# Attention in a one-core streaming encoder step: a place for each query block's probabilities, two blocks' scores in one piece, and stage A's transposes by 64 rows in an order by tiling mode

## The reference

```
layer A, prompt:  s = q k^T / 8, per head two components c (64 wide), mask by chunks of 64
                  p = softmax(s);  pd = p[c=0] - lam * p[c=1];  o = pd v   (v 128 wide)
layer A, streams: the same against 512 cached keys and 16 new ones, for 8 streams
                  o = rms_norm(o, g_sub) * 0.8;  x += o w_o
layer B, prompt:  s = q k^T / 8 + f_q - f_k, causal; p = softmax(s); o = p v  (16 heads of 64)
layer B, streams: the same against 512 cached keys and 16 new ones
```

## Time and profile before

| | |
|---|---|
| median of 3 runs | 2539.45 us (2537.55 to 2542.49) |
| the profiled execution | 2543.26 us |
| its span | 2541.5 us |
| PE busy | 2486.0 us, 98% of the span |
| PE weight loads busy | 2351.7 us, 93% |
| DVE busy | 1689.7 us, 66% |
| ACT busy | 1137.5 us, 45% |
| DMA | 271.42 MB, mean 107 GB/s |
| granted PE clock | 0.996 of full speed in the mean |

### The profile page before, as it was taken

The page is one execution under the profiler, slowest core; times in us unless marked ns, Lnnn a source line. Parts: engine busy times, 40 slices in busy tenths (PEclk is TensorE's granted clock), DMA queues, the critical chain, the costliest instruction groups (busy, mean ns, idle before and its releaser), DMA issues.

```text
span 2541.5 us, 46165 instructions
## 1 busy us (share of the span) xinstructions
PE 2486.0 (98%) x18533; PEld 2351.7 (93%) x18533; DVE 1689.7 (66%) x2953; ACT 1137.5 (45%) x2244; POOL 192.5 (8%) x136
## 2 busy tenths in 40 slices
PE   8999999999998999999999999999998899999998
PEld 8999999887777999999988999999985599999998
DVE  7777677331677877767634885868626677858585
ACT  6444344102775634344422543535427755435254
POOL 0000000543000000000054000000120000000000
PEclk9999999999999999999999999999999999999999
DMA  4323232234653222323224232322358731322222
GB/s 127 96 65 102 61 99 66 83 108 136 254 200 101 63 88 73 94 69 98 67 72 138 94 107 67 98 78 79 103 179 310 245 108 43 108 80 77 86 71 79
DMA packets 267136, 271.42 MB, mean 107 GB/s; under 512 B 13786, under 2 KB 224035, under 8 KB 266931
## 3 DMA queue, kind: packets, MB, share of 16 engines
q1 hardware_dynamic: 261184, 253.45, 32.0%
q10 hardware_dynamic: 5746, 15.12, 1.6%
HBM read 255.02 MB, written 13.51 MB: 106 GB/s over the span
## 4 chain that ended last, share of the span: by engine, by line
PE 89%; DVE 5%; ACT 4%; issue 2%; DMA 1%; DVEq 0%; SPq 0%; ACTq 0%
PE PS L775 40%; PE PS L881 24%; PE PS L962 10%; PE PS L725 6%; PE PS L708 2%; PE PS L1208 1%; PE PS L1016 1%; ACT R L1695 1%; PE PS L1147 1%; PE PS L713 1%; DMA R<-in_cache_b_k_dram 1%; ACT R L1727 1%; DVE x_area L2120 1%; PE PS L1168 1%; PE PS L1106 0%
## 5 line engine op out<-in xcount | busy, mean ns | idle before, releaser
L775 PE MATMUL PS<-x_area,w_area 128*128 128x320 f32 x3096 | 482.2, 309 | 0.0
L775 PEld LDWEIGHTS PS<-x_area,w_area 128*128 128x128 f32 x3096 | 461.1, 188 | 0.2 <-DVE w_area L2061 0.2
L881 PE MATMUL PS<-r_area,w_area 128*128 128x320 f32 x2568 | 393.4, 309 | 0.0
L881 PEld LDWEIGHTS PS<-r_area,w_area 128*128 128x128 f32 x2568 | 380.6, 188 | 0.8 <-DVE r_area L2253 0.8
L1482 ACT ACTIVATE w_area<-R 128x512 fp32r<-128x512 f32 x341 | 212.8, 628 | 201.1 <-PE PS L775 134.0
L2052 DVE TENSOR_TENSOR w_area<-R,w_area 128x768 fp32r<-128x768 f32 (+2 forms) x143 | 132.4, 926 | 220.3 <-ACT w_area L1467 218.7
L2061 DVE TENSOR_TENSOR w_area<-R,w_area 128x512 fp32r<-128x512 f32 x341 | 234.0, 687 | 47.4 <-ACT w_area L1482 41.5
L1467 ACT ACTIVATE w_area<-R 128x768 fp32r<-128x768 f32 (+2 forms) x143 | 117.0, 818 | 309.2 <-PE PS L881 281.2
L881 PE MATMUL PS<-v_area,w_area 128*128 128x320 f32 x1620 | 253.5, 309 | 0.0
L962 PE MATMUL PS<-w_area,xn_hi 128*128 128x512 f32 x800 | 251.0, 395 | 0.0
L881 PEld LDWEIGHTS PS<-v_area,w_area 128*128 128x128 f32 x1620 | 241.5, 188 | 0.3 <-DVE v_area L2253 0.3
(11 more groups left out here) (305 smaller groups left out, 3621.9 us busy)
## 6 DMA issues: line engine op xcount, KB each, us to landing
R<-in_w_ffn_up_dram SPq DMA_DIRECT2D x88, 512.0 KB, 3.8
R<-in_w_ffn_gate_dram SPq DMA_DIRECT2D x84, 512.0 KB, 3.9
R<-in_w_ffn_down_dram SPq DMA_DIRECT2D x96, 384.0 KB, 3.3
vreg<-in_cache_a_v_dram SPq DMA_DIRECT2D x8, 2048.0 KB, 8.9
vreg<-in_cache_b_v_dram SPq DMA_DIRECT2D x8, 2048.0 KB, 9.3
R<-in_cache_a_k_dram SPq DMA_DIRECT2D x14, 1024.0 KB, 5.8
R<-in_cache_b_k_dram SPq DMA_DIRECT2D x14, 1024.0 KB, 9.6
R<-in_w_qkv_a_dram SPq DMA_DIRECT2D x24, 512.0 KB, 3.8
```

Source lines behind the costliest of these rows:

```text
L775: last = pe.matmul(PS[:, bank, 0:HT], a[:, k, :], b[:, k, :], start=(start and k == 0 and a is hi and b is x_hi), stop=(k == 3 and a is lo ...
L881: last = pe.matmul(out[:, h, :], a[slot][:, w], x[:, h * HT:(h + 1) * HT], start=(k == 0 and a is w_hi and x is hi), stop=(k == n - 1 and ...
```

## The change

- `probs[x]` becomes a function of the block: each of the four blocks has a place of its own for probabilities, so `exps` no longer waits for the turn of an earlier block. `st` grows by two rows for the same reason, so that blocks 2 and 3 have their own statistics.
- The scores of blocks 0 and 1 of a head are written in one piece (columns 0 to 127 and 128 to 383 of banks 0 and 1), with one semaphore wait, and `peaks(h, (0, 1))` takes both with one `tensor_scalar`.
- Stage A turns probabilities (`turn`), stream differences (`stream_turn`, `stream_turn_new`) and cached keys (`key_pair`, two heads at once) by 64 rows, as B did. ACT takes half of A's `new_differences`. `keys`, `key` and `bank7_uses` go.
- The order of the steps changes on PE, ACT and DVE in both stages. In A PE does full-height work (`output_flips`, `output_rows`, `stream_flips`) in one group, then the 64-row work.
- Some semaphores are merged (`heads_read`, `pd_read`). SP's order is unchanged.

```diff
-        probs = {"A": R2[:, 4096:6144].rearrange("p (s c k) -> p s c k", s=2, c=2),
-                 "B": R2[:, 6144:8192].rearrange("p (s c k) -> p s c k", s=2, c=2)}
+        def probs(x, t):
+            at = {"A": 3584, "B": 6144}[x] + P * t * (t + 1)
+            return R2[:, at:at + 2 * P * (t + 1)].rearrange("p (c k) -> p c k", c=2)
+        def row_stats(t):
+            return st[:, t if t < 2 else t + 2, :]
+        def score_columns(t):
+            return slice(P, 3 * P) if t == 1 else slice(0, (t + 1) * P)
...
 PE, turn:
                     for c in parts:
                         for k in range(t + 1):
-                            block = PR[:, t % 2, c, k * P:(k + 1) * P]
-                            if x == "A":
-                                last = flip(PS[:, 5 + t % 2, k * P:(k + 1) * P], block)
-                                continue
                             at = (c * (t + 1) + k) * 64
                             for r in range(2):
-                                last = half_flip(PS[:, 5 + r, at:at + 64], block, r)
+                                last = half_flip(PS[:, 5 + r, at:at + 64], probs(x, t)[:, c, k * P:(k + 1) * P], r)
...
 PE, stream_turn and stream_turn_new:
+                def stream_block(to, g, k, r):
+                    p, rows = (t0, t1)[g][:, key_block(g, k)], slice(64 * r, 64 * r + 64)
+                    out = PS[:, 2 + 2 * r, to:to + 64]
+                    if x == "A":
+                        return pe.matmul(out, p[rows], Cm[rows, g, rows], start=True, stop=True)
+                    return half_flip(out, p, r)
...
 PE, order in A:
                     for i in range(PAIR):
                         stream_scores(i)
-                        keys(i + 1, 0)
-                        output_rows(i - 1, (0, 1, 2))
+                        output_flips(i - 2)
+                        output_rows(i - 1)
+                        stream_flips(i - 1)
+                        prompt_scores(x, i, (2,))
                         turn(i, 0)
-                        stream_flips(i - 1)
-                        scores(i, 1)
-                        keys(i + 1, 1)
-                        output_rows(i - 1, (3,))
-                        keys(i + 1, 2)
-                        scores(i, 2)
-                        keys(i + 1, 3)
+                        key_pair(i + 1, 0)
                         stream_turn(i)
-                        keys(i + 1, 4)
                         turn(i, 1)
-                        scores(i, 3)
+                        key_pair(i + 1, 1)
+                        prompt_scores(x, i, (3,))
                         stream_turn_new(i)
-                        keys(i + 1, 5)
                         turn(i, 2)
-                        keys(i + 1, 6)
+                        key_pair(i + 1, 2)
                         stream_values(i)
-                        keys(i + 1, 7)
-                        scores(i + 1, 0)
+                        key_pair(i + 1, 3)
+                        prompt_scores(x, i + 1, (0, 1))
                         turn(i, 3)
-                        output_flips(i - 1)
 ACT, order in A:
                     for i in range(PAIR):
+                        stream_roots(i - 1)
                         turned(i - 1, 3)
-                        exps(i, 0)
-                        stream_roots(i - 1)
-                        key(i + 1, 0)
-                        if i == 0:
-                            key(i + 1, 1)
+                        if i:
+                            exps(i, 0)
+                            exps(i, 1)
                         stream_exps(i)
-                        if i > 0:
-                            key(i + 1, 1)
-                        exps(i, 1)
+                        squares(i - 1)
                         turned(i, 0)
-                        key(i + 1, 2)
-                        squares(i - 1)
-                        key(i + 1, 3)
+                        key_pair(i + 1, 0)
+                        differences(i)
                         exps(i, 2)
+                        turned(i, 1)
                         roots(i - 1)
-                        differences(i)
-                        key(i + 1, 4)
-                        turned(i, 1)
-                        key(i + 1, 5)
+                        key_pair(i + 1, 1)
+                        new_differences(i)
                         turned(i, 2)
                         exps(i, 3)
-                        key(i + 1, 6)
+                        key_pair(i + 1, 2)
                         result(i)
-                        key(i + 1, 7)
+                        key_pair(i + 1, 3)
                         stream_squares(i)
 ACT, order in B (after):
                     for i in range(PAIR):
+                        turned(i - 1, 3)
+                        exps(i, 2)
                         stream_exps(i)
                         turned(i, 0)
                         key_pair(i + 1, 0)
-                        exps(i, 2)
                         differences(i)
...
                         exps(i + 1, 0)
+                        exps(i + 1, 1)
                         result(i)
                         key_pair(i + 1, 3)
 DVE, order in A:
                     for i in range(PAIR):
+                        stream_scale(i - 1)
+                        combine(i, 0)
+                        stream_peaks(i)
+                        combine(i, 1)
                         output_columns(i - 2)
-                        combine(i, 0)
-                        stream_scale(i - 1)
-                        stream_peaks(i)
+                        output_rows(i - 1)
                         stream_output(i - 1)
-                        peak(i, 1)
                         stream_norms(i)
-                        output_rows(i - 1)
-                        combine(i, 1)
-                        peak(i, 2)
+                        peaks(i, (2,))
+                        differences(i)
                         sums(i - 1)
-                        differences(i)
                         combine(i, 2)
                         scale_rows(i - 1)
-                        peak(i, 3)
+                        peaks(i, (3,))
                         new_differences(i)
                         combine(i, 3)
                         result(i)
-                        peak(i + 1, 0)
+                        peaks(i + 1, (0, 1))
 DVE, order in B:
                     for i in range(PAIR):
+                        peaks(i, (2,))
+                        stream_peaks(i)
                         combine(i, 1)
-                        stream_peaks(i)
+                        combine(i, 2)
                         output_columns(i - 1)
                         stream_output(i - 1)
-                        peak(i, 2)
                         stream_norms(i)
                         differences(i)
-                        combine(i, 2)
-                        peak(i, 3)
+                        peaks(i, (3,))
                         new_differences(i)
-                        peak(i + 1, 0)
+                        peaks(i + 1, (0, 1))
                         combine(i, 3)
+                        result(i)
                         combine(i + 1, 0)
-                        result(i)
-                        peak(i + 1, 1)
```

More of the change, by code:

```diff
@@ L1007, in first_keys, with prompt_scores @@
                 last.then_inc(sem("kt_ready" + x), 1)
-            def prompt_scores(x, h, t):
-                n = h * 4 + t
+            def prompt_scores(x, h, blocks):
+                if h == PAIR:
+                    return
+                n = h * 4 + blocks[0]
                 if n >= 1:
                     pe.wait_ge(sem(("exp_done" if x == "A" else "nb_ready") + x), n)
[L1014 to L1020, removed]
-                    if x == "A":
-                        last = pe.matmul(out, mask(M_EYE0, P, rows), mask(M_CHUNKED, P, rows), start=False, stop=True)
-                    else:
-                        pe.matmul(out, mask(M_EYE0, P, rows), mask(M_CAUSAL0, P, rows), start=False, stop=False)
-                        last = pe.matmul(out, mask(M_EYE1, P, rows), mask(M_CAUSAL1, P, rows), start=False, stop=True)
-                last.then_inc(sem("s_ready" + x), 1)
@@ new lines, in prompt_scores @@
+                for t in blocks:
+                    at = score_columns(t)
+                    for c in range(2):
+                        rows = slice(64 * c, 64 * c + 64)
+                        pe.matmul(PS[:, c, at], qh[rows, h, t * P:(t + 1) * P], kT[rows, h, 0:(t + 1) * P], start=True, stop=False)
+                    for c in range(2):
+                        rows = slice(64 * c, 64 * c + 64)
+                        out = PS[:, c, at.stop - P:at.stop]
+                        if x == "A":
+                            last = pe.matmul(out, mask(M_EYE0, P, rows), mask(M_CHUNKED, P, rows), start=False, stop=True)
+                        else:
```

(6 more changed lines are left out.)

297 lines of the change are left out of this document (108 added, 189 removed).

## The result

The changed kernel is slower: 2562.56 us in the median of 4 runs (2555.72 to 2564.06), against 2539.53 us for the kernel before on the same chip, a ratio of 1.0084 with a 95% interval of 1.0064 to 1.0105. The forecast was 2531 us, range 2517 to 2546: wrong in sign, and the time lies outside the range. The profiled execution took 2563.2 us.

What follows compares the result with a forecast made beforehand. PE was taken to be near its limit in stage A, and hand-offs to bound B. A -9.5 and B +1 make -8.5 us, 2534.8 from the profiled 2543.26, so 2531 us against the median; range 2517 to 2546.

Steps and rivals of the forecast that it cites:

- PE's work in A: falls by 4.0 us an iteration, from 18.9 to 14.9: First attention stage: half flips and fewer tiling-mode changes cut PE's busy time per iteration by 4.0 us.
- the bound of 0.056 us a pass: A's `stream_turn`: half of 0.112 us, no overlap, giving no gain; the prediction took 0.033 us, giving -0.9 us.
- keys and `turn`: PE in A, full flips to half flips: keys -1.5 us and `turn` -0.5 us per iteration.
- the 1.1 of the mode changes: PE in A: seven fewer tiling-mode changes per iteration at 0.16 us each, -1.1 us.
- The walk of A: 8.3 + 6.0 + 4.1 = 18.4: A's hand-offs from S (start of `stream_scores`) to the next S: period 18.4 us, -1.07 us per iteration.
- The middle term: A, from `stream_turn` to `stream_values`: 6.0 us after the change, 6.07 before.
- First iteration -2.8, last 0: A's ends: first iteration 2.8 us shorter, without earlier output in its path; last unchanged, at worst +0.5.
- B: +1 us: Second attention stage, where only the order moves: later `turn(i, 0)`, some stalls covered; +1 us, bounds -4 and +7.
- B loses more than A gains: Rival, chance 0.13: at `turn(i,0)` ACT is dry, B pays +13 us; with A at -5, 2547 us.
- Clock: Rival, chance 0.04: a quarter of PE's 119 us in A runs at 1.2 GHz, +20 us, 2550 us.
- Sum: Both attention stages: A -9.5 us plus B +1 us, -8.5 us in all.
- three engines at 14 us in 19.5: A after the change: PE, ACT and DVE each hold 14 to 15 us of 19.5, so hand-offs set the period.

Runs made afterwards that it cites:

- The plain turn: On the kernel with fillers, stage A's stream blocks turned by plain 64-row transposes, the product with `Cm` left out; 2537.95 us, ratio 0.9989.
- fillers: Changed kernel plus 128x128 matmuls that nobody reads, where TensorE is idle in both attention stages; 2550.27 us, ratio to before 1.0036.
- moving the two copies: Changed kernel with `output_columns` and `stream_output` directly behind `stream_peaks` on VectorE in B, ahead of two combines; 2548.38 us, ratio 1.0027.
- The last run: Changed kernel, B's old order, fillers at A's ends, block 2's exps first, A's DVE and ACT ordered by PE's waits; 2532.09 us, ratio 0.9963.

## Why the prediction was wrong, step by step

- *PE's work in A: falls by 4.0 us an iteration, from 18.9 to 14.9.* Direction right, size off. One iteration has 16.3 us of PE busy (690.20 to 710.09) where 18.9 stood. The keys came as forecast (sixteen half flips in 0.71 us). `stream_turn` gave nothing: 1.84 us from start to next against 1.79, forecast 0.9. The number of the bound of 0.056 us a pass was right and I chose the other one, on the ground that the operand shapes were the flips'; that bound's reason, no overlap, was not right, for two 64-row passes fit into the time of one full-height pass (0.116 us). Of the 2.6 us that PE's work fell, keys and `turn` were priced at 2.0, so some 0.6 are left for the 1.1 of the mode changes, which no run took apart.
- *The walk of A: 8.3 + 6.0 + 4.1 = 18.4.* Measured 8.52, 7.16 and 4.21. The middle term failed, by the 0.9 us of `stream_turn`; the rest of the walk was within 0.25 us a term. The plain turn bounds what it is worth: at most 0.92 us an iteration and 5.4 over the stage.
- *First iteration -2.8, last 0.* Measured +0.85 and +3.8. With fillers they are -1.9 and +1.8. So the clock took 2.7 us of the first and 2 of the last. The tail's chain is longer than I made it.
- *B: +1 us.* Measured +10. `turn(i, 0)` was forecast at 6.95 us after S and came at 7.28: the step that failed is not that time but its price. I counted the delay and left out that PE has nothing to do for it (2.23 us) and then works at 1.2 GHz. Filling the gap gives B 7.5 us back, moving the two copies 11.5. Even where the clock held behind the same wait the period was 18.25 us, above the 17.2 to 17.6 that were forecast, so the wait was under-priced as well as the clock.
- *The rivals.* "B loses more than A gains" named the place. Its condition, `turn(i, 0)` later than about 8 us after S, did not come true, and the loss was there at 7.28. "Clock" got 0.04, because in the earlier trace rows A was 97% busy and B had 0.98. But it is the gaps that the change makes which decide, not the share of before; half of the 23 us between the two medians was of this kind (12.3, by the fillers). That rival's own size, a quarter of A's work at the lower clock, is not what happened either: in A the clock was low in the first, the seventh and the last iteration, and in B, which the rival's price left out, it was low behind five of seven waits. It should have stood with the waits, in one sum: where the walk leaves PE idle, and at what clock the work behind runs. The walk itself said that PE would be idle 3.5 us of each iteration.
- *Sum.* A: forecast -9.5, measured +10.4. Of the 19.9 us between, 8.0 are clock (fillers) and at most 5.4 `stream_turn` (plain turn). Of the 6.5 or more that are left, 1.8 are the tail and 1.4 the instruction held beside POOL's product (with the fillers the seventh period is 1.8 us above its neighbours, before the change 0.45). The rest, the walk's small terms, was not taken apart.
- *What the new order was worth.* I took it that three engines at 14 us in 19.5 leave the hand-offs in charge and stopped there. The last run shows that the hand-offs could be moved. Its period of 17.18 us is shorter than the 18.86 that PE was busy in one iteration of the kernel before, so the smaller work on PE has a part in it; it had been hidden behind sums and row norms that nothing awaited. How much the new orders of DVE and ACT alone would have given the kernel before was not run.

What stays open: which pattern of short waits lowers the clock. The same waits did and did not. In the changed kernel the waits of 0.9, 1.2 and 1.5 us in A's middle did not lower it, but with the fillers one of 1.20 us at the same place did once in the middle of A, and block 3's scores took 1.96 us in place of 1.13:

```profile
680.17 1.96 PE L1015 MATMUL PS<-kT,R 64*128 64x512 f32 x4 [1.20 <-ACT R L1652]
```

The wait of 2.23 us in B lowered it five times in seven, and the group of 0.60, 0.16 and 0.95 us in four iterations. Open too are the waits on "issue" of 0.4 to 2.1 us in B, which are in every kernel and whose cause no run here tried.

## What to carry to other kernels

When an order is changed, list the idle times that the new order gives TensorE, and price the work behind each one at the lower clock as well. A filler that costs no path time tells in one run how much of a loss is clock. Where three engines wait for one another in a ring, move what nobody awaits behind what TensorE awaits, on VectorE and ScalarE: in this kernel the halved flips came with a gain only after that. And take a pass's price from a row of the same operation: here the fp32 products took two passes where the flips took one, each pass was dearer, and halving a product's output columns did not shorten its pass.

## What was unexpected in the hardware

- A pass of 128 rows by 64 columns of fp32 product takes 0.116 us, one of 128 by 128 takes 0.112. Two 64-row passes fit into that time (0.058 each).
- The same series of waits, to 0.01 us, kept the clock in one iteration and lost it in the next.
- A one-column DVE instruction took 2.00 us instead of 0.22 beside POOL's elementwise product of two 128 x 1024 operands. In four traces it ended 0.01 or 0.02 us behind that product, held for 2.00, 2.03, 0.65 or 0.42 us by where its order had put it. A `RECIPROCAL` on one column beside the same product took its usual 0.15 us.
- Work added to TensorE, some 0.11 us a pass in its idle time, made the changed program 12.3 us faster.
